# Modulation sums of an adaLN transformer: summed over partitions on TensorE beside the projections and kept on chip

## The chip, the cores and the metric

The kernel runs on one core of a Trainium2 chip. The engines of a core are named as in the profile: PE (TensorE), DVE (VectorE), ACT (ScalarE), POOL (GpSimd) and SP (SyncE, which here only issues DMAs). The metric is the device time of one execution in microseconds (us). Everything is computed in fp32.

## What is computed

512 tokens of width 1024 go through three layers: a first block (gated delta rule and spatial gating side by side, then a mixture of experts), a second layer with forgetting attention ("fox") and experts, and a third with latent attention (MLA) and experts. The second and third layer are modulated: a conditioning vector `c` gives, for each of the two layers, six rows of 1024 numbers:

```python
    c_act = jax.nn.silu(c)
    for i in range(DEPTH_2):
        mod = c_act @ w_ada[i] + b_ada[i]
        sh1, sc1, g1, sh2, sc2, g2 = [m[:, None, :] for m in jnp.split(mod, 6, axis=-1)]
        h = rmsnorm(x, mix_norm[i]) * (1.0 + sc1) + sh1
...
        x = x + g1 * y
        h = rmsnorm(x, ffn_norm[i]) * (1.0 + sc2) + sh2
        x = x + g2 * hier_moe(h, moe_w_grp[i], moe_b_grp[i], moe_w_rt[i], moe_b_rt[i],
                              moe_w_gate[i], moe_w_up[i], moe_w_down[i])
```

`y` is the attention of `h` (fox in layer 0, MLA in layer 1).

`w_ada[i]` is 1024 x 6144, 25 MB a layer. These sums depend on nothing but `c` and the weights, so they can be made at any time before the layer.

## The kernel before

**The sums.** Work is cut into 48 "slabs" a layer: six sums `m` times eight blocks `k` of 128 rows. A slab is a [128, 1024] piece of `w_ada` (512 KB) that SP loads (line 262) into one of four buffers (`NA = 4`: the `state` buffer, `ada_w` and two halves of a weight ring buffer, `ring_halves` in the trace). DVE multiplies it by a column of silu(c) and adds it to an accumulator of [128, 1024] (`sum_slab`, lines 282 and 286); two accumulators alternate. After eight slabs the accumulator holds, in each of its 128 partitions, a partial sum of one modulation row; the sum over the partitions is still to be taken. SP stores it to the scratch tensor `ada_part` in DRAM (line 266).

**Where they run.** Layer 0's slabs run beside two stages of the first block: 24 beside the u/v projections (block at line 521) and 24 beside the gate projections, the spatial mixing and the output projections (block at line 637). There DVE does twelve slabs before its "gated" step (line 738) and two behind each of the first six output jobs. Layer 1's 48 run beside the fox projections (from line 2361). A job is one 128-token by 512-column output, eight fp32 products of PE into one PSUM bank (lines 531, 651, 690, 2443). Weights come in chunks through a ring of buffers; SP issues a chunk (`W.issue`, line 120) as soon as the job that used the old one is done, from the same instruction stream as the slab loads, in the order that `move_slabs` sets.

**Stages.** Each `nc.Block()` holds one instruction stream for each engine and ends with a barrier of all engines. Named steps (`PE.done`, `DV.wait` and so on) are counts on one semaphore per engine.

**The way back.** In each of the two expert stages ahead of a modulated layer, SP reloads the six partial sums (`modulation_loads`, from line 1272), and DVE adds the bias in four adds of one partition by 1536 (line 1922). In the combine stage (`Combine.sums`, line 2044) PE sums over the partitions: eight products of a full block of ones with 512 columns give the four rows that are needed in all partitions (line 2047; "rows"), and 16 products of 128x128 with one column give sh1 and sc1 as columns (line 2053; "cols"). DVE copies the columns (line 2117) and makes the scales (lines 2119, 2122); PE's `turn(0)`, the transposes (line 2072), waits for these and for ACT's normed rows (line 2099).

## Time and profile before

| | us |
|---|---|
| median of 3 runs | 2089.75 |
| lowest, highest | 2088.21, 2093.47 |
| span of the profiled execution | 2089.7 |
| PE busy in it | 2004.7 |
| DVE busy | 965.4 |
| ACT busy | 441.4 |
| POOL busy | 361.3 |

The profiled execution is as long as the median run. A "busy" figure says how long an engine worked, not whether anyone waited for it; for that the rows below give windows of single stages, and timelines with the idle time before an instruction and its releaser in square brackets. A row of a timeline may join several equal instructions (x4); an fp32 product of PE shows as two records.

### The profile page before, as it was taken

What the parts mean: (1) busy time and instruction counts of PE and PEld (TensorE: products, weight loads), DVE (VectorE), ACT (ScalarE), POOL (GpSimd) and SP (SyncE); (2) the same over time, 40 slices, a digit from 0 to 9 for tenths busy, and PEclk for the clock granted to TensorE, in tenths of its full rate; (3) what the DMA queues carried; (4) which work ended last, traced back from release to release, by engine and by line L of the source; (5) the groups of instructions that cost most, each with busy time, mean ns of one, the idle gap of its engine ahead of it and who ended that gap; (6) DMA issues with size and microseconds to landing.
All of it is one profiled execution on the core that took longest, in us unless ns stands there. A gap on an engine that the chain in (4) does not pass through costs nothing. (4 is left out here: it accounts for less than half of the span.)

```text
span 2089.7 us, 20494 instructions
## 1 busy us (share of the span) xinstructions
PE 2004.7 (96%) x7434; PEld 1071.0 (51%) x7434; DVE 965.4 (46%) x1776; ACT 441.4 (21%) x1063; POOL 361.3 (17%) x540
## 2 busy tenths in 40 slices
PE   8999999999999999999899999999998999999995
PEld 4444444578874444444445446454445557544442
DVE  3444534567673024333454556253344467444333
ACT  1112111023241001100241126220004446320000
POOL 1000000000002000334200026103331003203333
PEclk9999999999999999999998999999999999999997
DMA  6223365610022134699715861138994120046996
GB/s 197 81 97 131 115 248 181 212 72 2 1 65 91 66 103 161 227 408 401 293 63 210 323 220 52 44 140 318 402 393 169 64 103 1 3 161 224 373 379 243
DMA packets 125750, 367.53 MB, mean 176 GB/s; under 512 B 28028, under 2 KB 33432, under 8 KB 113104
## 3 DMA queue, kind: packets, MB, share of 16 engines
q1 hardware_dynamic: 79744, 177.28, 23.9%
q10 hardware_dynamic: 30432, 157.30, 19.3%
q0 software_dynamic: 15472, 31.61, 4.3%
q8 instruction: 62, 1.02, 0.2%
q14 instruction: 40, 0.33, 0.0%
HBM read 339.79 MB, written 43.55 MB: 183 GB/s over the span
## 5 line engine op out<-in xcount | busy, mean ns | idle before, releaser
L1640 PE MATMUL bank<-ring,work 128*128 128x512 f32 x768 | 340.3, 596 | 3.3 <-DVE work L1656 3.3
L1640 PEld LDWEIGHTS bank<-ring,work 128*128 128x128 f32 x768 | 143.1, 191 | 166.7 <-issue 166.7
L1939 POOL DMA_INDIRECT work<-x_rows,small x168 | 169.6, 1010 | 267.2 <-DVE work L1904 202.6
L1651 PE MATMUL bank<-ring_halves,work 128*128 128x512 f32 x384 | 172.8, 593 | 4.0 <-DVE work L1665 4.0
L2443 PE MATMUL bank<-ring,featT 128*128 128x512 f32 x384 | 170.0, 603 | 1.6 <-DVE small L2535 1.6
L1368 PE MATMUL bank<-ring,work 128*128 128x512 f32 x384 | 168.2, 598 | 3.0 <-PEq L1184 1.0
L432 PE MATMUL bank<-featT,ring 128*128 128x512 f32 x384 | 168.7, 593 | 2.4 <-DMA ring<-in_w_in 2.4
L1662 DVE TENSOR_TENSOR work<-work,bank 128x256 f32<-128x256 f32 x48 | 20.2, 421 | 280.1 <-ACT work L1659 280.1
L2443 PEld LDWEIGHTS bank<-ring,featT 128*128 128x128 f32 x384 | 73.9, 194 | 93.9 <-issue 92.2
L1651 PEld LDWEIGHTS bank<-ring_halves,work 128*128 128x128 f32 x384 | 72.7, 190 | 95.1 <-issue 95.1
L1368 PEld LDWEIGHTS bank<-ring,work 128*128 128x128 f32 x384 | 72.8, 192 | 92.3 <-issue 92.3
L432 PEld LDWEIGHTS bank<-featT,ring 128*128 128x128 f32 x384 | 71.2, 190 | 83.3 <-issue 80.8
L531 PE MATMUL bank<-ring,featT 128*128 128x512 f32 x256 | 110.4, 593 | 0.9 <-PEq L412 0.9
L1659 ACT ACTIVATE work<-bank 128x256 f32<-128x256 f32 x48 | 18.4, 384 | 412.6 <-PE bank L1640 412.6
L1904 DVE STREAM_TRANSPOSE work<-work 128x1024 f32<-128x1024 f32 x42 | 85.1, 2027 | 0.0
L1085 PE MATMUL bank<-ring,featT 128*128 128x512 f32 x192 | 83.3, 593 | 1.0 <-PEq L815 1.0
L531 PEld LDWEIGHTS bank<-ring,featT 128*128 128x128 f32 x256 | 48.5, 190 | 61.4 <-issue 61.4
L286 DVE SCALAR_TENSOR_TENSOR ring_halves<-ring_halves,ismall 128x1024 f32<-128x1024 f32 x48 | 61.6, 1283 | 37.6 <-DMA ring_halves<-in_w_ada 34.1
L453 DVE TENSOR_SCALAR work<-bank,small 128x512 f32<-128x512 f32 x24 | 18.0, 751 | 105.3 <-PE bank L432 105.3
L1085 PEld LDWEIGHTS bank<-ring,featT 128*128 128x128 f32 x192 | 36.1, 190 | 44.7 <-issue 44.7
L1193 PE MATMUL bank<-ring,work 128*128 128x512 f32 x128 | 55.5, 593 | 0.9 <-PEq L1074 0.9
L690 PE MATMUL bank<-ring,work 128*128 128x512 f32 x128 | 55.3, 592 | 0.0
(472 smaller groups left out, 2859.2 us busy)
## 6 DMA issues: line engine op xcount, KB each, us to landing
ring<-in_w_in SPq DMA_DIRECT2D x15, 2048.0 KB
ring<-in_moe_w_gate ACTq DMA_DIRECT2D x28, 1024.0 KB
ring<-in_moe_w_up ACTq DMA_DIRECT2D x28, 1024.0 KB
ring_halves<-in_moe_w_down ACTq DMA_DIRECT2D x28, 1024.0 KB, 10.2
ring_halves<-in_w_ada SPq DMA_DIRECT2D x48, 512.0 KB, 6.9
y_rows<-work ACTq DMA_DIRECT2D x48, 512.0 KB
ring<-in_expert_w_gate ACTq DMA_DIRECT2D x14, 1024.0 KB
ring<-in_expert_w_up ACTq DMA_DIRECT2D x14, 1024.0 KB
```

Source lines behind the costliest of these rows:

```text
L286: DV.done(nc.vector.scalar_tensor_tensor(out=acc, in0=w, scalar=c_cols[:, k:k + 1], in1=acc, op0=ALU.mult, op1=ALU.add), ("slab", i))
L432: last = nc.tensor.matmul(bank[b % 4][:, :], w[:, k, (b % 4) * P:(b % 4 + 1) * P], featT[:, k, :], start=(k == 0), stop=(k == KD - 1))
L531: last = nc.tensor.matmul(uv_bank(j)[:, :], featT[:, k, t * P:(t + 1) * P], w[:, k, :], start=(k == 0), stop=(k == KD - 1))
L690: last = nc.tensor.matmul(six(16 + j)[:, :], gatedT[:, t, k, :], w[:, k, :], start=(k == 0), stop=(k == KD - 1))
L1085: last = nc.tensor.matmul(zg_bank(j)[:, :], featT[:, k, t * P:(t + 1) * P], w[:, k, :], start=(k == 0), stop=(k == KD - 1))
L1193: last = nc.tensor.matmul(bank[j][:, :], oT[:, k, t * P:(t + 1) * P], w[:, k, :], start=(k == 0), stop=(k == KD - 1))
L1368: last = nc.tensor.matmul(bank[j % 4][:, :], outT[:, k, t * P:(t + 1) * P], w[:, k, :], start=(k == 0), stop=(k == KD - 1))
L1640: last = nc.tensor.matmul(gu_sum[par], xgT[par][:, k, :], w_gu[par][:, k, :, :], start=(k == 0), stop=(k == KD - 1))
L1651: last = nc.tensor.matmul(bank[5 + h][:, :], hT[par][:, k, :], w_dn[par][:, k, span(h)], start=(k == 0), stop=(k == KF - 1))
L1904: nc.vector.transpose(xgT[par].rearrange("p k (s b) -> p s k b", s=NQ), xg[par].rearrange("p (s a k) -> p s k a", s=NQ, k=KD)).then_inc(M_ ...
L1939: nc.gpsimd.indirect_dma_start(out=xg[par][:, s * QD:(s + 1) * QD], out_offset=None, in_=x_quarters, in_offset=bass.IndirectOffsetOnAxis(a ...
L2443: last = nc.tensor.matmul(f_bank(j)[:, :], featT[:, k, t * P:(t + 1) * P], w[:, k, :], start=(k == 0), stop=(k == KD - 1))
```

## The change

The sum over partitions is taken at once, beside the projections. After certain jobs PE multiplies each half of a finished accumulator by a 32-column block of ones (`mod_sum`): two products of [128, 512] into 32 PSUM partitions each, of bank 0 (bank 7 in the fox stage, whose projections now rotate through six banks instead of seven). So every row arrives in 32 equal copies. DVE adds the bias to 64 partitions x 512 (`keep_mod`) and keeps the result in a small on-chip tensor (`mod_all`, 1040 columns) or, for sh1 and sc1, in a piece of a work buffer. The bias was loaded there before by eight DMAs of POOL (`load_mod_bias`). POOL turns sh1 and sc1 into columns with 16 DMAs of 128 elements a layer (`store_mod_cols`). The scratch tensor, its stores and reloads, the bias adds of the expert stages and the column products of the combine stages are gone. The rows of the combine stage are products with one partition of ones. `ada_w` is no longer a buffer, so slabs go through three (`NA = 3`); the position of the weight chunks among the slab loads moves by up to one slab with it. In the fox stage the slabs run over jobs 4 to 21 instead of 4 to 23.

```diff
-        ada_w = [state, sb("ada_w", [P, KD * P]), ring[3][:, 0:DM], ring[3][:, DM:2 * DM]]
+        ada_w = [state, ring[3][:, 0:DM], ring[3][:, DM:2 * DM]]
...
+        mod_rows = mod_all[:, 0:2 * BANK].rearrange("p (b n) -> p b n", b=2)
+        sh_cols, sc_cols = (mod_all[:, 2 * BANK + KD * i:2 * BANK + KD * (i + 1)] for i in range(2))
...
-        def store_sum(eng, i):
-            l, q = i // SLABS, i % SLABS // KD
-            eng.dma_start(ada_part[l, :, q * DM:(q + 1) * DM], ada_acc(i)).then_inc(ada_stored[i // KD % 2], 16)
 
...
             if k == 0:
                 if i >= 2 * KD:
-                    dve.wait_ge(ada_stored[i // KD % 2], 16 * (i // KD // 2))
+                    dve.wait_ge(PE.sem, mod_summed[i // KD - 2])
...
-                if j >= NA and beside[j - NA] % KD == KD - 1:
-                    store_sum(sp, beside[j - NA])
                 for _ in range(issue_after.count(j)):
                     W.issue(sp, 1)
-            if n and (beside[-1] + 1) % SLABS == 0:
-                for stored in ada_stored:
-                    sp.wait_ge(stored, 16 * SUMS // 2 * (beside[-1] // SLABS + 1))
+
+        def mod_sum(pe, m, b):
+            pe.wait_ge(DV.sem, slab_at[m * KD + KD - 1])
+            for h in range(2):
+                lo = 32 * (2 * (m % 2) + h)
+                last = nc.tensor.matmul(b[lo:lo + 32, :], ones[:, 0:32], ada_acc(m * KD)[:, span(h)], start=True, stop=True)
+            PE.done(last, ("mod", m))
+
+        def mod_half(m, cols):
+            q = m % SUMS
+            rows_ = slice(64 * (q % 2), 64 * (q % 2) + 64)
+            return cols[rows_, :] if q < COL_SUMS else mod_rows[rows_, (q - COL_SUMS) // 2, :]
+
+        def keep_mod(dve, m, b, cols):
+            out = mod_half(m, cols)
+            dve.wait_ge(PE.sem, mod_summed[m])
+            dve.wait_ge(mod_bias_landed[m // SUMS], 16 * 8)
+            DV.done(nc.vector.tensor_tensor(out, b[64 * (m % 2):64 * (m % 2) + 64, :], out, ALU.add), ("mod", m))
+
+        def load_mod_bias(eng, l, cols):
+            bias = D["b_ada_2"][l:l + 1, :]
+            for j in range(4):
+                eng.dma_start(cols[32 * j:32 * j + 32, :], bias[:, j * BANK:(j + 1) * BANK].partition_broadcast(32)).then_inc(mod_bias_landed[l], 16)
+                eng.dma_start(mod_rows[32 * j:32 * j + 32, :, :],
+                              bias[:, COL_SUMS * DM:].rearrange("o (b j n) -> o j b n", b=2, j=4)[:, j, :, :].partition_broadcast(32)).then_inc(mod_bias_landed[l], 16)
+
+        def store_mod_cols(eng, l, cols):
+            for m in range(l * SUMS, l * SUMS + COL_SUMS):
+                eng.wait_ge(DV.sem, mod_kept[m])
+            for i, to in enumerate((sh_cols, sc_cols)):
+                for k in range(KD):
+                    row = 32 * (2 * i + k // 4)
...
+        mod_after = {7: 0, 12: 1}
...
+                    if j in mod_after:
+                        AC.wait(pe, "beta")
+                        DV.wait(pe, "dt")
+                        mod_sum(pe, mod_after[j], bank[0])
...
-                for i in beside:
+                for i in beside[:2 * KD]:
                     sum_slab(dve, i, beside)
+                keep_mod(dve, 0, bank[0], mod_cols)
+                for i in beside[2 * KD:]:
+                    sum_slab(dve, i, beside)
+                keep_mod(dve, 1, bank[0], mod_cols)
+
+            @block.gpsimd
+            def _(pool):
+                load_mod_bias(pool, 0, mod_cols)
+                store_mod_cols(pool, 0, mod_cols)
...
+        MOD_AT = 1
+        mod_out = {2: 3, 3: 4, 7: 5}
...
+        mod_kept_at = {3: 3, 5: 4, 7: 5}
...
+                pe.wait_ge(DV.sem, mod_kept[1])
...
+                    if j == MOD_AT:
+                        DV.wait(pe, ("spT", 0))
+                        mod_sum(pe, 2, bank[0])
...
+                    if j in mod_out:
+                        AC.wait(pe, ("kept", T - 1))
+                        if mod_out[j] == 5:
+                            DV.wait(pe, ("mod", 3))
+                        mod_sum(pe, mod_out[j], bank[0])
...
-            for stored in ada_stored:
-                sp.wait_ge(stored, 16 * SUMS // 2 * (l + 1))
-            for i in range(SUMS):
-                paced(i)
-                load(sp, ada_sum[:, i * DM:(i + 1) * DM], ada_part[l, :, i * DM:(i + 1) * DM])
-            paced(SUMS)
...
-                        if mod is not None and BIAS_AT <= e < BIAS_AT + 4:
-                            i = e - BIAS_AT
-                            part = ada_sum[32 * i:32 * i + 1, i * B_ADA:(i + 1) * B_ADA]
-                            dve.wait_ge(loaded, mod_loads)
-                            DV.done(nc.vector.tensor_tensor(part, part, b_ada[32 * i:32 * i + 1, :], ALU.add), ("bias", i))
...
-                    at = ROW_OF[i][1] * DM + ROW_OF[i][2] * BANK
-                    PE.done(nc.tensor.matmul(row_bank(i)[:, :], ones[:, :], ada_sum[:, at:at + BANK], start=True, stop=True), ("row", i))
-                pe.wait_ge(loaded, self.rows.mod_loads)
+                    at = 2 * (ROW_OF[i][1] - COL_SUMS) + ROW_OF[i][2]
+                    p = 32 * (at % 4)
+                    PE.done(nc.tensor.matmul(row_bank(i)[:, :], ones[p:p + 1, :], mod_rows[p:p + 1, at // 4, :], start=True, stop=True), ("row", i))
+                pe.wait_ge(DV.sem, mod_kept[SUMS * self.rows.mod + SUMS - 1])
                 for i in range(2, len(ROW_OF)):
                     row(i)
-                for q in range(2):
-                    for k in range(KD):
-                        last = nc.tensor.matmul(bank[0][:, q * KD + k:q * KD + k + 1], ada_sum[:, q * DM + k * P:q * DM + (k + 1) * P], ones[:, 0:1], start=True, stop=True)
-                PE.done(last, "cols")
                 row(0)
...
-                dve.wait_ge(PE.sem, PE.value("cols"))
-                DV.done(nc.vector.tensor_copy(small[:, 80:80 + 2 * KD], bank[0][:, 0:2 * KD]), "cols")
-                dve.wait_ge(DV.sem, DV.value("cols"))
+                dve.wait_ge(norm_landed[self.rows.mod], 16 * (KD + 1))
+                dve.wait_ge(mod_cols_landed, 16 * COL_SUMS * KD * (self.rows.mod + 1))
...
-        f_bank = lambda j: bank[1 + j % 4] if j < 8 else bank[1 + j % 7]
-        bank_user = lambda j: j - 4 if j < 8 else {8: 5, 9: 6, 10: 7, 11: 7, 12: 7, 13: 7, 14: 4}.get(j, j - 7)
+        f_bank = lambda j: bank[1 + j % 4] if j < 8 else bank[1 + j % 6]
+        bank_user = lambda j: j - 4 if j < 8 else {8: 6, 9: 7, 10: 7, 11: 7, 12: 4, 13: 5}.get(j, j - 6)
...
-        part = lambda j: beside[SLABS * max(0, j - SLABS_AT) // (len(jobs) - SLABS_AT):SLABS * max(0, j + 1 - SLABS_AT) // (len(jobs) - SLABS_AT)]
+        SLAB_JOBS = len(jobs) - SLABS_AT - 2
+        by_job = lambda j: min(SLABS, SLABS * max(0, j - SLABS_AT) // SLAB_JOBS)
+        part = lambda j: beside[by_job(j):by_job(j + 1)]
+        mod_bank, mod_cols = bank[7], work[:, FOX_END:FOX_END + BANK]
+        mod_after = {next(j for j in range(len(jobs)) if by_job(j) >= KD * (q + 1)): SUMS + q for q in range(SUMS)}
+        mod_kept_at = {min(j + 1, len(jobs) - 1): m for j, m in mod_after.items()}
...
+                    if j in mod_after:
+                        m = mod_after[j]
+                        if m >= SUMS + 2:
+                            DV.wait(pe, ("mod", m - 2))
+                        mod_sum(pe, m, mod_bank)
...
+                PE.wait(pool, ("row", 1))
+                DV.wait(pool, ("bias", T - 1))
+                load_mod_bias(pool, 1, mod_cols)
...
+                AC.wait(pool, ("kept", T - 1, 3))
+                DV.wait(pool, ("kept", T - 1, 7))
+                store_mod_cols(pool, 1, mod_cols)
```

In the u/v stage PE's stream had sixteen jobs in a row (here jobs 6 to 13; `ring` is the weight buffer, `featT` the tokens).

Before:

```order
L531 MATMUL bank7<-ring1,featT 128x512 x8
L531 MATMUL bank1<-ring1,featT 128x512 x8
L531 MATMUL bank2<-ring0,featT 128x512 x8
L531 MATMUL bank3<-ring0,featT 128x512 x8
L531 MATMUL bank4<-ring0,featT 128x512 x8
L531 MATMUL bank5<-ring0,featT 128x512 x8
L531 MATMUL bank6<-ring1,featT 128x512 x8
L531 MATMUL bank7<-ring1,featT 128x512 x8
```

After:

```order
L573 MATMUL bank7<-ring1,featT 128x512 x8
L573 MATMUL bank1<-ring1,featT 128x512 x8
L315 MATMUL bank0<-ring_halves,ones 32x512 x2
L573 MATMUL bank2<-ring0,featT 128x512 x8
L573 MATMUL bank3<-ring0,featT 128x512 x8
L573 MATMUL bank4<-ring0,featT 128x512 x8
L573 MATMUL bank5<-ring0,featT 128x512 x8
L573 MATMUL bank6<-ring1,featT 128x512 x8
L315 MATMUL bank0<-ring_halves,ones 32x512 x2
L573 MATMUL bank7<-ring1,featT 128x512 x8
```

Two pairs of 32-column products now stand behind jobs 7 and 12; each waits for DVE's last slab of its sum, and the following job is queued behind it.

POOL had nothing in the u/v and gate stages. Before, from its last stores of the stage ahead to the delta rule (`y_rows` is another scratch tensor):

```order
L487 DMA y_rows<-work 128x1024 [waits pe_steps,pool_steps]
L487 DMA y_rows<-work 128x1024 [waits pe_steps] x6
L412 UNCONDITIONAL_BRANCH
L1031 UNCONDITIONAL_BRANCH [waits barrier_Pool_Activation_PE_DVE_SP_gather]
L1033 MEMSET state 128x1024
```

After (the four pairs of bias loads are cut to two):

```order
L450 UNCONDITIONAL_BRANCH
L631 UNCONDITIONAL_BRANCH [waits barrier_Pool_Activation_PE_DVE_SP_gather]
L332 DMA work<-in_b_ada_2 32x512
L333 DMA mod_all<-in_b_ada_2 32x2x512
...
L332 DMA work<-in_b_ada_2 32x512
L333 DMA mod_all<-in_b_ada_2 32x2x512
L342 DMA mod_all<-work 128x1x1 [waits dve_steps]
L342 DMA mod_all<-work 128x1x1 x15
L563 UNCONDITIONAL_BRANCH
L1106 UNCONDITIONAL_BRANCH [waits barrier_Pool_Activation_PE_DVE_SP_gather]
L1108 MEMSET state 128x1024
```

The bias loads and the 16 column stores now stand between two barriers; the first column store waits for DVE's two kept sums.

PE's stream in the fox combine (`work` holds the reloaded sums, `mod_all` the kept rows). Before:

```order
L2047 MATMUL bank6<-work,ones 128x512
L2053 MATMUL bank0<-ones,work 128x1 x16
L2047 MATMUL bank7<-work,ones 128x512
L2047 MATMUL bank1<-work,ones 128x512
L2062 MATMUL bank2<-level_mask,ident 128x512 x2
L2072 MATMUL bank5<-ident,work 128x128 x4
L2072 MATMUL bank6<-ident,work 128x128 x4
```

After:

```order
L2103 MATMUL bank6<-mod_all,ones 128x512
L2103 MATMUL bank7<-mod_all,ones 128x512
L2103 MATMUL bank1<-mod_all,ones 128x512
L2114 MATMUL bank2<-level_mask,ident 128x512 x2
L2124 MATMUL bank5<-ident,work 128x128 x4
```

The 16 column products between the rows are gone, and the transposes (`bank5<-ident,work`) follow the same rows as before.

## Rows read from the trace of the kernel before

**Rows 1.** The page's first part: busy us, share of the span, instructions by engine

```profile
PE 2004.7 (96%) x7434; PEld 1071.0 (51%) x7434; DVE 965.4 (46%) x1776; ACT 441.4 (21%) x1063; POOL 361.3 (17%) x540
```

**Rows 2.** Windows of three stages: us, busy (x) by engine, PEclk, DMA share, GB/s

```profile
199.00:309.00 110.00, 109.95 (x259) 48.80 (x260) 58.28 (x57) 14.75 (x28) 0.00 (x0) 1.00 0.53 189
865.00:970.00 105.00, 105.00 (x261) 47.30 (x260) 33.89 (x40) 9.82 (x20) 39.98 (x40) 1.00 1.01 396
1055.00:1233.00 178.00, 176.45 (x475) 86.09 (x473) 91.26 (x103) 33.58 (x73) 2.76 (x5) 0.96 0.63 225
```

**Rows 3.** Groups by line and form: line engine op, out<-in, shapes, count | busy us, mean ns

```profile
L531 PE MATMUL bank<-ring,featT 128*128 128x512 f32 x256 | 110.4, 593 | 0.9 <-PEq L412 0.9
...
L442 PE MATMUL bank<-featT,work 128*16 128x512 f32 x16 | 7.0, 593 | 0.0
```

**Rows 4.** Timeline of PE, second attention heads: start us, us, line, op, count

```profile
1252.95 1.13 PE L2671 MATMUL bank<-work 64*128 64x512 f32 x4
1254.02 0.44 PE L2680 MATMUL bank<-ident,ring_halves 128*128 128x128 f32 x2
```

**Rows 5.** Timeline of POOL from the first projections to the delta rule

```profile
435.51 0.95 POOL L1033 MEMSET state<- 128x1024 f32 x1 [266.48 <-POOLq L637]
```

**Rows 6.** Timeline of all engines where the u/v stage ends

```profile
309.73 0.60 ACT L603 ACTIVATE work<-bank 128x512 f32<-128x512 f32 x1 [6.27 <-PE bank L531]
...
310.64 1.06 PE L642 MATMUL bank<-ident,resid 128*128 128x128 f32 x8 [0.94 <-PEq L521]
```

**Rows 7.** Timeline of SP's queue in the u/v stage

```profile
282.26 0.38 SPq L120 DMA_DIRECT2D ring<-in_w_in  x1
...
296.18 1.72 SPq L262 DMA_DIRECT2D ring_halves<-in_w_ada  x2
```

**Rows 8.** Timeline of DVE in the u/v stage

```profile
294.86 2.67 DVE L286 SCALAR_TENSOR_TENSOR ring_halves<-ring_halves,ismall 128x1024 f32<-128x1024 f32 x2 [11.53 <-DMA ring_halves<-in_w_ada]
...
301.39 2.67 DVE L286 SCALAR_TENSOR_TENSOR ring_halves<-ring_halves,ismall 128x1024 f32<-128x1024 f32 x2
```

**Rows 9.** Timeline of POOL in the fox stage

```profile
1179.16 2.21 POOL L2362 DMA_DIRECT2D work<-key_rows  x4 [5.31 <-DMA key_rows<-work]
```

**Rows 10.** Timeline of all engines, MLA combine

```profile
1591.25 3.98 PE L2053 MATMUL bank<-ones,work 128*128 128x1 f32 x32
...
1591.97 0.95 POOL L2036 DMA_INDIRECT work<-y_rows,ismall  x1 [0.30 <-issue]
...
1593.22 0.94 POOL L2036 DMA_INDIRECT work<-y_rows,ismall  x1 [0.30 <-issue]
...
1598.95 1.15 ACT L2099 ACTIVATE work<-resid,small 128x1024 f32<-128x1024 f32 x1
...
1601.18 1.94 PE L2072 MATMUL bank<-ident,work 128*128 128x128 f32 x8 [2.33 <-DVE work L2122]
```

**Rows 11.** Timeline of DVE in the gate stage

```profile
363.23 1.28 DVE L286 SCALAR_TENSOR_TENSOR ring_halves<-ring_halves,ismall 128x1024 f32<-128x1024 f32 x1 [5.39 <-DMA ring_halves<-in_w_ada]
364.50 0.75 DVE L282 TENSOR_SCALAR ring_halves<-state,ismall 128x1024 f32<-128x1024 f32 x1
...
370.43 4.22 DVE L738 SCALAR_TENSOR_TENSOR work<-bank,small,work 128x128 f32<-128x128 f32 x16
```

**Rows 12.** Timeline of PE in the gate stage

```profile
371.60 0.66 PE L662 MATMUL bank<-ident,work 128*128 128x128 f32 x4 [1.39 <-DVE work L738]
```

**Rows 13.** Slab loads (line 262), all of the run

```profile
DMA to landing us min/median/max: 3.5/6.8/15.7
```

**Rows 14.** Timeline of DVE in the fox stage

```profile
1189.29 1.28 DVE L286 SCALAR_TENSOR_TENSOR ring_halves<-ring_halves,ismall 128x1024 f32<-128x1024 f32 x1 [4.29 <-DMA ring_halves<-in_w_ada]
...
1221.38 1.28 DVE L286 SCALAR_TENSOR_TENSOR ring_halves<-ring_halves,ismall 128x1024 f32<-128x1024 f32 x1 [5.27 <-DMA ring_halves<-in_w_ada]
```

**Rows 15.** Timeline of PE, fox combine

```profile
1030.46 3.63 PE L2053 MATMUL bank<-ones,work 128*128 128x1 f32 x32
...
1042.95 1.94 PE L2072 MATMUL bank<-ident,work 128*128 128x128 f32 x8 [3.63 <-ACT work L2099]
```

More of the change, by code:

```diff
@@ L57, in wait @@
         eng.wait_ge(self.sem, self.value(name, i))
[L60 removed]
+Rows = namedtuple("Rows", "nth index late w1 w2 mod y_in early")
 class Weights:
@@ L274, in take_slabs, with mod_names, note_steps @@
             return beside
+        def mod_names(*which):
+            return [("mod", m) for m in which]
+        def note_steps(beside, summed, kept):
+            for i in beside:
+                slab_at[i] = DV.value(("slab", i))
+            for m in summed:
+                mod_summed[m] = PE.value(("mod", m))
+            for m in kept:
+                mod_kept[m] = DV.value(("mod", m))
         def sum_slab(dve, i, beside):
@@ L317, in links @@
             return [(name, i) for i in range(n)]
-        def span(t, half=BANK):
-            return slice(t * half, (t + 1) * half)
         x_tok = D["x"][0].rearrange("(t p) n -> p t n", p=P)
@@ L519, in build @@
         ac_names = ["ab", "beta", "log_beta", "exp", "rate"] + [(s, i) for i in range(2) for s in ("log", "inv")] + ["log"] + [("drained",) + j for j in jobs]
-        stage([("sum",) + jobs[0]] + ["ab"] + [("sum",) + j for j in jobs[1:]], ac_names, dv_names + slab_names(beside))
+        mod_after = {7: 0, 12: 1}
+        mod_cols = buf[5][:, 7 * BANK:8 * BANK]
+        uv_pe = [x for j, job in enumerate(jobs) for x in [("sum",) + job] + (["ab"] if j == 0 else []) + (mod_names(mod_after[j]) if j in mod_after else [])]
+        stage(uv_pe, ac_names, dv_names + slab_names(beside[:2 * KD]) + mod_names(0) + slab_names(beside[2 * KD:]) + mod_names(1))
+        note_steps(beside, (0, 1), (0, 1))
         with nc.Block() as block:
@@ L620, in build @@
         vrstd = small[:, 128 + 14 * T:128 + 15 * T]
-        pe_names = [("spT", h) for h in range(2)] + [("sum",) + j for j in gate_jobs]
+        MOD_AT = 1
+        mod_out = {2: 3, 3: 4, 7: 5}
+        pe_names = [("spT", h) for h in range(2)] + [x for j, job in enumerate(gate_jobs) for x in [("sum",) + job] + (mod_names(2) if j == MOD_AT else [])]
         for t in range(T + 1):
@@ L625, in build @@
             pe_names += [("turned", t - 1, h) for h in range(2)] if t else []
[L626 to L627 removed]
+        pe_names += [x for j in range(OUT_EARLY, 2 * T) for x in [("out",) + gate_jobs[j]] + (mod_names(mod_out[j]) if j in mod_out else [])]
+        dv_names = [("spT", h) for h in range(2)] + [(w, t) for t in range(T) for w in ("half0", "half1")] + [("mean", t) for t in range(T)] + ["eps"] + mod_names(2)
         dv_names += [(w, t) for t in range(T) for w in ("gain", "bias")] + slab_names(beside[:12])
@@ L1333, in moe @@
             dv_n += links("route", N_ROUTE) + links("pick", N_PICK) + links("rows", N_ROWS)[:ROWS_FIRST] + ["slot_tok", "skip", "slot_f"] + links("rows", N_ROWS)[ROWS_FIRST:] + ["part_f", "part_rows"] + links("weight", N_WEIGHT)
-            dv_n += [("bias", i) for i in range(4)] if mod is not None else []
-            BIAS_AT = NE - 4
             stage([("sum", j) for j in range(6)] + [("turned", 0, 0), ("turned", 0, 1), ("sum", 6), ("turned", 1, 0), ("turned", 1, 1), ("sum", 7)] +
@@ L1996, in sum_names @@
             def sum_names(self):
-                return [("row", i) for i in range(2, len(ROW_OF))] + ["cols", ("row", 0), ("row", 1)]
+                return [("row", i) for i in range(2, len(ROW_OF))] + [("row", 0), ("row", 1)]
             def turn_names(self, t):
```

52 lines of the change are left out of this document (31 added, 21 removed).

## The prediction

> **What bounds the kernel now.** I read the busy table first: TensorE (PE) is busy for 2004.7 of 2089.7 us, 96% [rows 1]. Such a share is a mean over stages, so next come windows over the stages that the change touches. In the u/v projection stage PE is busy for 109.95 of 110.00 us, and in the projections of the first attention layer (fox) for 176.45 of 178.00; the clock is granted at or close to full, the DMA engines are at 0.53 and 0.63 of their time and DVE is at about half [rows 2]. So whatever is put on PE there lengthens the run by its own duration, and whatever is taken from DVE or the DMA queues gives nothing. The expert stage, from which the change takes six reloads, is also 105.00 of 105.00 PE, but its DMA share is 1.01 at 396 GB/s: two candidates for its pace [rows 2].
>
> **Part 1: twelve sums over partitions on PE.** Each is a pair of fp32 products of a 32-column block of ones with 512 columns, put on different column groups of the array. The trace has no 32-column product. An ordinary 512-column product is two records of 110.4/256 = 0.43 us, and a 16-column-wide one costs the same, 7.0/16 = 0.44 a record [rows 3]: narrowness alone saves nothing. What can save is that the pair runs side by side. The nearest row is the attention's pair of 64-row tiles with 512 columns: four records start at 1252.95 and the next instruction starts at 1254.02, 1.07 us for what would be 4 x 0.43 = 1.72 in a row [rows 4]. I take 1.07, as it is also a pair of 512 columns in separate parts of the array, entered from and left to full-size products. The ends are 0.86 (perfect overlap) and 1.72 (none). All twelve stand between projection or output jobs of stages where PE has no idle time, so all of it counts: 12 x 1.07 = **+12.8** (10.3 to 20.6).
> The Trainium skill, page "TensorEngine Tiling (Array Packing)", section Key Properties, says that changing the tiling mode, not just the tile, drains TensorE; the 0.21 us by which the pair of [rows 4] exceeds 0.86 would be that drain. Its page "TensorE: Matmul & The Clock Gate", section "Measured speedup vs the span model", gives a pack of tiles the time of one product plus some ns for each further tile; by that the pair would be an estimated 0.86 and the total 2106.8.
>
> **Part 2: the end of the u/v stage.** Every stage ends with a barrier of all engines. Before, POOL has nothing there (idle for 266.48 us before 435.51) and the last drain of ACT, 309.73 + 0.60, releases PE at 310.64 [rows 5, 6]. Now POOL waits there for the second kept sum, which stands on DVE behind slab 23, and then issues 16 small DMAs in front of the barrier. With three buffers slab 23 is later. The weight chunk that SP issues at 282.26 waits for a projection job, and only behind it go the loads of slabs 18 and on [rows 7]; DVE then waits until 294.86 [rows 8]. One product moves this to 295.9. Slabs 18 to 20 are summed until 299.9 (1.28 and a gap of 0.1 each). The load of 23 now needs the buffer of 20; before, with four buffers, the pair issued at 296.18 was summed from 301.39 on, so a landing took some 5 us [rows 7, 8]. So 23 lands at about 305.2, is summed at 306.5, and the bias add (64 x 512) ends at 307.2. The 16 issues go by POOL's direct DMAs: four in 2.21, so 0.55 each [rows 9]: 8.8, end 316.0. PE and ACT themselves come to 310.33 + 2 x 1.07 = 312.5. The tail is **+3.5** (0 if slab and issues run ahead; +14.7 if an issue takes the 1.25 us that separates the indirect ones, 1591.97 to 1593.22 [rows 10]).
>
> **Part 3: three slab buffers in the gate stage.** The mixing of the first token tile waits for DVE, which does twelve slabs first: they end as DVE's "gated" step begins, 370.43, and PE idles 1.39 for it [rows 11, 12]. The last five slabs come in a burst from 363.23. With three buffers the last two of the five are only issued when the first two are summed, at 364.5 and 365.2, and take the slabs' median landing of 6.8 us [rows 13]: one after the other summed by 374.2 (371.6 + 2 x 1.28), 3.7 later, of which one product on PE (1.07) covers a part: 2.6. By the shortest landing, 3.5, nothing is lost. Fewer loads in flight make each somewhat quicker, so I take **+2.0** (0 to 2.6).
>
> **Part 4: PE's waits for slabs in the fox stage.** PE now waits at six places for the eighth slab of a sum, with the next projection job queued behind it. The slabs end one job (about 7 us) ahead of each product, which hides most. Against it: DVE already waits for landings of up to 4.29 and 5.27 there [rows 14], six weight chunks block SP in between, and there is one buffer less. I estimate four of six late by half a us or so, **+2.3**; 0 if the spare job covers all, 9.6 if two are late by those two waits.
>
> **Part 5: the combine stages.** The 16 column products (32 records) go: 3.63 and 3.98 us of PE [rows 10, 15]. In the fox one PE then waits 3.63 anyway for ACT's normed rows (1042.95): gain 0 [rows 15]. In the MLA one PE waits until 1601.18 for DVE's scale rows, which stood behind the column products; ACT is done at 1598.95 + 1.15 = 1600.10, and that is late next: **-1.0** [rows 10]. The row products stay eight, each with one row of ones instead of 128; the time goes with the columns, so I give them nothing.
>
> **Part 6: what costs or gives nothing.** The eight bias adds on DVE in the expert stages, 12 stores and 12 reloads lie beside PE work that fills the stages [rows 2]. The twelve adds on DVE replace them. POOL's stores for the second layer are issued in the fox stage after its key rows, around 1182, and need 8.8 us: over long before the stage ends.
>
> **Sum.** 12.8 + 3.5 + 2.0 + 2.3 - 1.0 = +19.6, on the profiled execution's 2089.7, which is the median of the runs (2089.75): **2109.3**. This case by itself spans 2103 to 2114.
>
> **Rivals.**
> (a) The pair runs one product after the other, as two records of 0.43 each in a row do [rows 3]: 12 x 0.65 = 7.8 more, 2117.1. For it: they use the same rows and the same moving port. Against: the pair of row tiles does overlap [rows 4]. 0.10.
> (b) POOL's issues cost 1.25 each: 11.2 more, 2120.5. For: they write single elements to 128 partitions. Against: its direct DMAs take 0.55 [rows 9]. 0.11.
> (c) Three buffers set the pace of the fox stage: 9.6 in place of 2.3, 2116.6. 0.06.
> (d) Faster, the other side: the DMA engines, not PE, pace the two expert stages. The reloads are 6 x 0.52 = 3.1 MB in each, 7.9 us at 396 GB/s. If both give that back, both column blocks count (7.6) and none of the new stalls appears: 2089.7 + 12.8 - 15.9 - 7.6 = 2079.0. It decides from the point where PE would have idle time in that stage; it has none there, 105.00 of 105.00 [rows 2]. 0.04.
> (e) No change to speak of: the relief comes in one expert stage only and the stalls stay hidden: 2089.7 + 12.8 - 7.9 - 1.0 = 2093.6. Nearly the same time results if the products do not do what they say and slip into PE's gaps; the 0.05 us of idle in the u/v stage leaves no gaps [rows 2]. 0.07.
> The forecast keeps 0.62.
>
> **How the numbers follow.** About 0.3%, 6.3 us, is what can be told from no change. Faster 0.04 (d), same 0.07 (e), slower the rest, 0.89. All terms at their low ends give 2089.7 + 10.3 - 1.0 = 2099.0; I set the low end at 2096, where case (e) begins, and the high end at 2122, over (a), (b) and (c) each alone. Left out are (d), (e) and two of the high cases together, 0.15.
>
> **What would show it.** The profile after: 48 records of ones products with 32 columns on PE, and 1.07 us from the first record of a pair to the next job (0.86 or 1.72 for the ends); the u/v stage about 5.6 longer, with POOL's last column store ending after ACT's last drain; PE's idle time before the first mixing transposes grown from 1.39 to about 3.4; small idle entries before the fox products with DVE's slab sums as releaser; PE waiting for ACT, not DVE, before the MLA combine's transposes; the expert stage unchanged at 105.00 of PE work. What would make the prediction wrong: a shorter expert stage, column stores that take over 1 us each, or pairs that don't overlap.

## The result, and the profile after

The changed kernel took 2125.87 us (median of 4, 2122.04 to 2130.73) against 2088.98 for the kernel before (2083.9 to 2093.47): a ratio of 1.0182, interval 1.0159 to 1.0206. It is slower by 36.9 us, where +19.6 was forecast; the time lies 4 us above the range.

The page's first part of the changed kernel, which answers to [rows 1] (2004.7 us, 96%):

```profile
span 2128.7 us, 20503 instructions
...
PE 2009.1 (94%) x7418; PEld 1063.9 (50%) x7418; DVE 959.4 (45%) x1778; ACT 440.4 (21%) x1063; POOL 380.9 (18%) x588
```

The span is 39.0 longer, PE's busy time only 4.4: the new products and half-speed stretches came on, the column products went, and so did most of the time of the row products. PE waits 34.6 us more. Some 16 of these stand in the two combine stages, where they fill the place of products that are gone (below); the others lengthen the run, and they are what to look for. The first PE instruction behind each stage barrier gives the length of the stages (differences of such starts, in us; three of the experiments below stand beside):

| stage | before | changed | stores later | ten slabs | before, three buffers |
|---|---|---|---|---|---|
| u/v projections | 111.60 | 123.62 | 113.95 | 113.95 | 111.59 |
| gate, mixing, output | 124.91 | 136.98 | 133.92 | 127.22 | 129.85 |
| delta rule (first part) | 181.28 | 181.28 | 181.28 | 181.29 | 181.28 |
| first experts | 259.05 | 260.46 | 257.32 | 257.16 | 257.52 |
| fox combine and projections | 210.64 | 217.83 | 219.96 | 219.43 | 214.49 |
| last experts to the end | 280.56 | 285.41 | 284.89 | 281.15 | 283.90 |

+12.0, +12.1 and +7.2 in the three stages that hold the products: 31.3. The other 7.7 us stand elsewhere: 4.9 in the last stage, 1.9 ahead of the u/v stage, 1.4 in the first experts, -0.5 in the rest. The profile of before has the shortest last stage of all eleven profiles, and the granted clock says most of why. Windows, columns as in [rows 2], first of before, then of the changed kernel:

```profile
1809.14:2065.00 255.86, 250.24 (x698) 117.86 (x698) 93.78 (x154) 22.44 (x50) 68.93 (x86) 1.00 0.72 267
...
1927.20:1934.00 6.80, 5.97 (x11) 2.50 (x10) 4.24 (x19) 2.30 (x4) 4.02 (x4) 0.50 0.13 38
```

The changed kernel has a stretch of 6.8 us at half speed in the last stage, before has none there. PE is busy for 5.97 of it, so it costs 3.0 of the 4.9. Such a stretch also stands in the last stage of two kernels that are before with a small edit (1895.0 to 1901.9 and 1900.9 to 1907.7); it is not shown to come from the change.

**The end of the u/v stage.** Timeline of all engines of the changed kernel, in answer to [rows 6] (PE went on at 310.64, idle 0.94):

```profile
308.88 8.63 POOL L342 DMA_DIRECT2D mod_all<-work  x16 [103.31 <-DVE work L327]
314.02 0.60 ACT L658 ACTIVATE work<-bank 128x512 f32<-128x512 f32 x1 [6.27 <-PE bank L573]
314.08 0.38 SPq L120 DMA_DIRECT2D ring<-in_w_in  x1
...
324.60 1.94 PE L702 MATMUL bank<-ident,resid 128*128 128x128 f32 x8 [10.62 <-PEq L563]
```

POOL's 16 issues end at 317.51, ACT's drain at 314.62, and yet PE goes on at 324.60, 7.1 us after that; in these no engine works. The column stores' own rows of the last two issues say when their data arrived (6.1 us behind the issue, 323 for the last):

```profile
L342 POOL DMA_DIRECT2D mod_all<-work x2: 544/544/544, 316.4 to 317.0; - x2
...
DMA to landing us min/median/max: 5.9/6.1/6.3
```

**The clock behind the waits.** Windows of the changed kernel, columns as in [rows 2]:

```profile
201.00:311.00 110.00, 110.00 (x262) 47.90 (x263) 59.61 (x59) 14.71 (x28) 6.27 (x12) 1.00 0.55 181
316.00:324.00 8.00, 0.00 (x0) 0.00 (x0) 0.00 (x0) 0.00 (x0) 1.51 (x3) 0.51 0.68 236
324.00:328.00 4.00, 3.40 (x10) 2.44 (x11) 2.11 (x4) 1.28 (x1) 0.00 (x0) 0.50 0.65 202
328.00:330.00 2.00, 2.00 (x4) 0.87 (x3) 2.00 (x4) 0.00 (x0) 0.00 (x0) 0.56 0.98 401
392.00:398.00 6.00, 6.00 (x28) 5.68 (x29) 5.16 (x19) 0.60 (x1) 0.00 (x0) 0.50 1.04 400
891.00:996.00 105.00, 105.00 (x261) 47.22 (x260) 33.86 (x40) 9.80 (x20) 39.73 (x40) 1.00 0.99 367
```

The granted clock is 0.50 (1.2 of 2.4 GHz) until about 330, after a wait of 10.6 us, and again from 392 to 398, after one of 4.1. PE counts as busy there, at half speed. The expert stage is what it was, 105.00 of 105.00 PE, with 367 GB/s instead of 396.

**The gate stage.** DVE and PE, from two timelines, in answer to [rows 11, 12] (gated step at 370.43, PE idle 1.39):

```profile
379.65 1.28 DVE L299 SCALAR_TENSOR_TENSOR ring_halves<-state,ismall,ring_halves 128x1024 f32<-128x1024 f32 x1 [5.75 <-DMA state<-in_w_ada]
...
390.79 4.22 DVE L807 SCALAR_TENSOR_TENSOR work<-bank,small,work 128x128 f32<-128x128 f32 x16
```

```profile
341.87 1.05 PE L315 MATMUL bank<-ring_halves,ones 128*32 128x512 f32 x4
342.85 41.47 PE L711 MATMUL bank<-ring,featT 128*128 128x512 f32 x96
...
391.96 2.15 PE L725 MATMUL bank<-ident,work 128*128 128x128 f32 x8 [4.08 <-DVE work L807]
393.90 3.62 PE L736 MATMUL bank<-work,resid 128*128 128x128 f32 x16
```

From the first record of a pair to the next product it is 342.85 - 341.87 = 0.98 us. That is not yet the price of a pair: the records on both sides of it also stand further apart (0.52 and 0.53 instead of 0.43), and the first experiment gives 1.18 from the length of a stage. PE then waits 4.08 for DVE's gated step, which waits for slabs; the 16 records that took 1.95 take 3.62.

**The MLA combine**, PE's timeline, in answer to [rows 10]:

```profile
1635.32 1.94 PE L2124 MATMUL bank<-ident,work 128*128 128x128 f32 x8 [10.35 <-ACT work L2151]
1637.05 3.58 PE L2114 MATMUL bank<-level_mask,ident 128*128 128x512 f32 x4
1640.47 4.05 PE L2947 MATMUL bank<-ring,featT 128*128 128x288 f32 x16
```

**The fox stage**, PE's waits ahead of its products, two rows of PE's timeline:

```profile
1215.51 1.05 PE L315 MATMUL bank<-ring_halves,ones 128*32 128x512 f32 x4 [1.88 <-DVE small L2620]
...
1237.97 1.05 PE L315 MATMUL bank<-ring_halves,ones 128*32 128x512 f32 x4 [0.62 <-DVE ring_halves L299]
```

At 1215.51 the profile names L2620, DVE's instruction just behind the last slab; that slab itself had waited 1.12 for its load. The other four pairs are not waited for.

The granted clock falls in this stage in both kernels, at the same place, with PE busy all the time. Before, then the changed kernel:

```profile
1109.70:1123.30 13.60, 13.60 (x46) 10.40 (x46) 0.74 (x1) 0.00 (x0) 0.00 (x0) 0.50 0.41 142
...
1138.70:1148.90 10.20, 10.20 (x35) 7.62 (x35) 1.29 (x1) 0.00 (x0) 0.00 (x0) 0.50 0.34 106
```

The stretch is 3.4 us shorter in the changed kernel, which gives back 1.7. Its combine also brings the first job 0.5 earlier (22.44 us behind the stage's start instead of 22.91).

### The profile page after: what moved, and what is told of

Read it like the earlier page. It is cut to its first block and busy times, and to the rows that moved or that the text cites. A ratio compares the mean times of both kernels' runs of the same rounds, so it can differ in the third digit from the quotient of the medians.

```text
span 2128.7 us, 20503 instructions
## 1 busy us (share of the span) xinstructions
PE 2009.1 (94%) x7418; PEld 1063.9 (50%) x7418; DVE 959.4 (45%) x1778; ACT 440.4 (21%) x1063; POOL 380.9 (18%) x588
## 5 line engine op out<-in xcount | busy, mean ns | idle before, releaser
L1702 PE MATMUL bank<-ring,work 128*128 128x512 f32 x768 | 345.8, 604 | 3.3 <-DVE work L1718 3.3
L2502 PE MATMUL bank<-ring,featT 128*128 128x512 f32 x384 | 169.8, 601 | 1.6 <-DVE small L2599 1.6
L1430 PE MATMUL bank<-ring,work 128*128 128x512 f32 x384 | 166.5, 593 | 3.0 <-PEq L1259 1.1
L573 PE MATMUL bank<-ring,featT 128*128 128x512 f32 x256 | 110.9, 594 | 0.9 <-PEq L450 0.9
L299 DVE SCALAR_TENSOR_TENSOR ring_halves<-ring_halves,ismall 128x1024 f32<-128x1024 f32 x56 | 71.8, 1282 | 34.0 <-DMA ring_halves<-in_w_ada 31.2
L1160 PE MATMUL bank<-ring,featT 128*128 128x512 f32 x192 | 83.3, 592 | 1.0 <-PEq L888 1.0
L299 DVE SCALAR_TENSOR_TENSOR ring_halves<-state,ismall,ring_halves 128x1024 f32<-128x1024 f32 x28 | 35.9, 1283 | 58.9 <-DMA state<-in_w_ada 57.8
L711 PE MATMUL bank<-ring,featT 128*128 128x512 f32 x128 | 57.1, 607 | 0.0
```

The costliest lines, as they stand in the source:

```text
L299: DV.done(nc.vector.scalar_tensor_tensor(out=acc, in0=w, scalar=c_cols[:, k:k + 1], in1=acc, op0=ALU.mult, op1=ALU.add), ("slab", i))
L573: last = nc.tensor.matmul(uv_bank(j)[:, :], featT[:, k, t * P:(t + 1) * P], w[:, k, :], start=(k == 0), stop=(k == KD - 1))
L711: last = nc.tensor.matmul(six(j)[:, :], featT[:, k, t * P:(t + 1) * P], w[:, k, :], start=(k == 0), stop=(k == KD - 1))
L1160: last = nc.tensor.matmul(zg_bank(j)[:, :], featT[:, k, t * P:(t + 1) * P], w[:, k, :], start=(k == 0), stop=(k == KD - 1))
L1430: last = nc.tensor.matmul(bank[j % 4][:, :], outT[:, k, t * P:(t + 1) * P], w[:, k, :], start=(k == 0), stop=(k == KD - 1))
L1702: last = nc.tensor.matmul(gu_sum[par], xgT[par][:, k, :], w_gu[par][:, k, :, :], start=(k == 0), stop=(k == KD - 1))
```

## The experiments

The theory after the two traces: (A) POOL does not reach the stage barrier before its own small DMAs have landed, and these share the DMA engines with the 2 MB weight chunk; (C) three slab buffers hold up DVE in the gate stage; (E) the products take 0.98 a pair, from the first record to the next product, since column groups overlap; and each PE wait of some us costs as much again in half-speed clock.

### Column stores in the gate stage

```diff
             def _(pool):
                 load_mod_bias(pool, 0, mod_cols)
-                store_mod_cols(pool, 0, mod_cols)
...
+            @block.gpsimd
+            def _(pool):
+                store_mod_cols(pool, 0, mod_cols)
```

The added lines stand in the gate stage's block.

> The changed kernel with one edit: the 16 column stores of the second layer's modulation (POOL) are issued in the gate stage and no longer in the u/v stage. Theory A (the tail of the u/v stage is POOL's alone): PE's idle time before the gate stage falls from 10.6 to about 1 us, and the slow clock after it (17.3 us for what took 14.7) goes with it: 9.7 + 2.6 = 12.3 us, so about 2113.6 us, a ratio to the kernel before of 1.012. Rival B (the stage end waits for something else that the change brought, such as the later slabs or SP's weight chunk): the idle time stays above 5 us and the run above 2119 us.

Measured: 2112.62 (2112.26 to 2114.68), ratio 1.0118, interval 1.0087 to 1.0149; 13.3 under the changed kernel. Its timeline of all engines:

```profile
312.63 1.06 PE L701 MATMUL bank<-ident,resid 128*128 128x128 f32 x8 [0.94 <-PEq L563]
...
313.16 4.96 POOL L342 DMA_DIRECT2D mod_all<-work  x9 [109.87 <-POOLq L563]
```

The wait is back at 0.94 and the half-speed stretch is gone (L701 takes 1.06, not 1.94). The u/v stage is 113.95 against 111.60 before, both with 0.94 of idle time at its end: its two pairs cost 2.35, 1.18 each. Theory A stands: the whole tail was the column stores.

### The weight chunk behind the barrier

```diff
-                move_slabs(sp, beside, [NA - 1] + spread(24, 3))
-                W.issue(sp)
+                move_slabs(sp, beside, [NA - 1] + spread(24, 3)[:2])
...
+                W.issue(sp, 1)
                 move_slabs(sp, beside, spread(24, 4))
```

> The changed kernel with the 2 MB weight chunk, which SP issues at the end of the u/v stage, issued as the first instruction of the gate stage. The changed kernel's last column store ends at 317.5 and PE goes on at 324.6, 7.1 us later. Theory A1 (POOL's stream reaches the barrier only when its own small DMAs have landed, and these lie in the DMA engines behind the 2 MB chunk): the 7.1 falls to 2 to 3 us. Rival A2 (each store really costs POOL about 0.96 us, 16 x 0.96 = 15.4 from 308.9 to 324.3, whatever the trace shows): it stays at 7. Rival A3 (a fixed time of POOL behind its last store): it stays at 7.

Measured: one run, 2115.34. Timeline of all engines, and the landing of the last two stores:

```profile
308.77 8.63 POOL L342 DMA_DIRECT2D mod_all<-work  x16 [103.34 <-DVE work L327]
...
320.02 0.38 SPq L120 DMA_DIRECT2D ring<-in_w_in  x1
...
320.08 1.94 PE L701 MATMUL bank<-ident,resid 128*128 128x128 f32 x8 [6.25 <-PEq L563]
```

```profile
DMA to landing us min/median/max: 1.9/1.9/1.9
```

From the last issue's end, 317.40, to PE it is 2.7 us and no longer 7.1, as A1 said. POOL's 16 issues are the same, so neither a hidden price of the issue (A2) nor a fixed time behind it (A3) explains the 7.1. What changed is the landing: 1.9 us instead of 6.1.

### Half of the stores

Eight column stores in the u/v stage, eight in the gate stage:

```diff
                 load_mod_bias(pool, 0, mod_cols)
-                store_mod_cols(pool, 0, mod_cols)
+                store_mod_cols(pool, 0, mod_cols, (0,))
...
+                store_mod_cols(pool, 0, mod_cols, (1,))
```

> The changed kernel with 8 of the 16 column stores in the u/v stage and the other 8 in the gate stage. The 8 start about 308.9 and their last ends about 313.3; ACT's last drain ends at 314.6 and the weight chunk moves data from 315 on. Theory A1 (landing behind the chunk): they have landed before it, and PE goes on at 315 to 315.5, idle about 1 to 1.5 us. A2 (0.96 us each): POOL is through at 316.6, PE goes on at about 316.9. A3 (fixed 7 us behind the last store): 320.3.

Measured: one run, 2128.26. None of the three numbers came: DVE was later here, so the stores started at 310.52 and ended behind the chunk's issue.

```profile
310.52 4.35 POOL L343 DMA_DIRECT2D mod_all<-work  x8 [105.44 <-DVE work L327]
...
313.57 0.38 SPq L120 DMA_DIRECT2D ring<-in_w_in  x1
...
322.02 1.94 PE L703 MATMUL bank<-ident,resid 128*128 128x128 f32 x8 [8.54 <-PEq L564]
```

```profile
DMA to landing us min/median/max: 6.1/6.4/6.7
```

Read by the mechanism and not by the numbers: the last two stores, issued up to 314.3, took 6.1 and 6.7 to land, 321.0, and PE went on at 322.02. Half as many stores shorten the wait by 2.1 us only (8.54 against 10.62). A2, counted from the real start, would give 318.2. By itself this run can't tell A1 from A3; with the one before it can.

### One small DMA in the kernel before

```diff
+            @block.gpsimd
+            def _(pool):
+                AC.wait(pool, ("drained",) + jobs[-1])
+                pool.dma_start(probe[:, :], ident[0:1, :]).then_inc(probed, 16)
```

> The kernel before with one small DMA more and nothing else: in the u/v stage POOL waits for ACT's last drain (310.3) and writes 128 numbers of 4 bytes to a scratch tensor, in front of the stage's barrier; SP has issued the 2 MB weight chunk 0.6 us earlier. Theory A1 (POOL reaches the barrier only when its own DMA has landed, here behind the chunk): PE, which went on at 310.6 before, goes on at 317 to 321. Rival A3 in a mild form (POOL only needs the 0.55 us of the issue): at 311.2 to 311.5.

Measured: one run, 2103.24. All engines, and the landing of the added DMA, then of the chunk:

```profile
311.34 0.38 SPq L120 DMA_DIRECT2D ring<-in_w_in  x1
311.35 0.60 ACT L605 ACTIVATE work<-bank 128x512 f32<-128x512 f32 x1 [6.27 <-PE bank L533]
312.23 0.52 POOL L610 DMA_DIRECT2D probe<-ident  x1 [141.60 <-ACTq L523]
...
319.90 1.94 PE L649 MATMUL bank<-ident,resid 128*128 128x128 f32 x8 [8.60 <-PEq L523]
```

```profile
DMA to landing us min/median/max: 7.3/7.3/7.3
...
DMA to landing us min/median/max: 11.0/11.0/11.0
```

A single transfer of 512 bytes holds all five engines for 7.6 us: issued at 312.23, landed at 319.5, PE on at 319.90, against 0.94 of idle time without it. This is theory A alone, in the kernel before.
Nobody waits for the semaphore of that DMA. The Trainium skill, page "DMA: Bandwidth & Descriptors", section "Queues, rings and completion order", says that a DMA engine takes turns between queues packet by packet; so a small transfer need not wait for the whole chunk. Here it did not: issued 0.9 us behind the chunk, it landed at 319.5, some 2.8 us ahead of it. But its 7.3 us are far from the 1.9 of the stores without a chunk; what held it for that long, no run here shows.

### The stores issued by ACT

The 16 stores stand on ACT between its last two drains, with a semaphore of their own:

```diff
                 for j, (n, t) in enumerate(jobs):
+                    if j == len(jobs) - 1:
+                        store_mod_cols(act, 0, mod_cols)
                     PE.wait(act, ("sum", n, t))
```

> The changed kernel with the 16 column stores of the u/v stage issued by ACT instead of POOL, between its last two drains (16 issues of some 0.35 us from about 308.3, through at 314), with a semaphore of their own; they still stand in front of the stage's barrier, and the last of them still land behind the start of the 2 MB chunk. Theory A4 (only POOL's own DMAs hold its way to the barrier; those that ACT issues through a hardware queue do not): PE goes on at 315 to 316.5, idle 1 to 2.5 us in place of 10.6, and the run is near the 2112.6 of the first experiment. Rival A5 (the barrier waits for small DMAs of any engine, or for this transfer): PE goes on at 322 to 325.

Measured: 2124.85 (2119.97 to 2127.55), ratio 1.0174, interval 1.0141 to 1.0208. All engines, and the landing of the last two stores:

```profile
308.83 12.49 ACTq L342 DMA_DIRECT2D mod_all<-work  x16
...
321.37 0.60 ACT L659 ACTIVATE work<-bank 128x512 f32<-128x512 f32 x1 [14.12 <-issue]
...
322.28 1.94 PE L703 MATMUL bank<-ident,resid 128*128 128x128 f32 x8 [8.80 <-PEq L563]
```

```profile
DMA to landing us min/median/max: 5.0/5.2/5.4
```

The time by PE (322.28) looks like rival A5, but the rows say something else. The issues took 12.49 / 16 = 0.78 us each, not 0.35, so ACT's own drain is late, 321.97. PE goes on 0.3 us behind that, while the last store, issued about 320.7, lands only near 326. So transfers that ACT issues do not hold the barrier; these were dear for another reason, their issue. The expected gain missed by the issue price.

### Both products of a pair on one column group

```diff
-                lo = 32 * (2 * (m % 2) + h)
+                lo = 32 * (2 * (m % 2))
```

> The changed kernel with both 32-column products of a pair on the same column group (the same 32 PSUM partitions; the second overwrites the first, so half of each modulation row is lost and the output is wrong). In the changed kernel a pair takes 0.98 us from its first record to the next instruction. Theory E (they take 0.98 because two column groups run side by side): now 1.7 to 1.8. Rival F (a 32-column product is simply cheaper, 0.25 a record): still 0.98.

Measured, PE's timeline:

```profile
256.84 1.90 PE L315 MATMUL bank<-ring_halves,ones 128*32 128x512 f32 x4
258.68 34.60 PE L573 MATMUL bank<-ring,featT 128*128 128x512 f32 x80
```

1.84 for the pair instead of 0.98 (one run, 2139.44). Theory E: the two column groups do run side by side, and that saves 0.86 a pair. The stage agrees: its length less PE's wait at its end is 114.72 (127.50 - 12.78) against 113.00 (123.62 - 10.62), 0.86 for each of its two pairs.

### Narrow products

```diff
-                last = nc.tensor.matmul(b[lo:lo + 32, :], ones[:, 0:32], ada_acc(m * KD)[:, span(h)], start=True, stop=True)
+                last = nc.tensor.matmul(b[lo:lo + 32, 0:16], ones[:, 0:32], ada_acc(m * KD)[:, h * BANK:h * BANK + 16], start=True, stop=True)
```

> The changed kernel with the 24 products over 16 columns of the accumulator in place of 512 (the rest of each modulation row is not computed; same waits, same order). Theory G (the products cost their own duration, 12 x 0.98 = 11.8, on top of everything else): with some 0.1 to 0.2 left for each pair, 9.5 to 10.5 us less than the changed kernel, about 2116. Rival H (the products fall partly into time that PE would wait anyway, for slabs in the fox and gate stage): 7 us less or fewer.

Measured: 2117.89 (2113.68 to 2121.93), ratio 1.0126, interval 1.0096 to 1.0156: 8.0 less than the changed kernel, between the two theories.

```profile
255.89 0.24 PE L315 MATMUL bank<-ring_halves,ones 128*32 128x16 f32 x4
256.06 34.60 PE L573 MATMUL bank<-ring,featT 128*128 128x512 f32 x80
```

A pair is 0.17 now, so 12 x 0.81 = 9.7 are gone from PE. In this profile the u/v tail was 2.2 us longer (idle 12.82), and in the fox stage the clock fell at one more place, so only part shows. By its median the run does not decide between G and H. The u/v stage does for its two pairs: its length less the wait at its end is 111.39 (124.21 - 12.82) against 113.00, 0.81 less a pair, that is in full, as G says. The waits for slabs in the fox stage stayed what they were (2.37 and 0.54 against 1.88 and 0.62), which also speaks against H.

### Three buffers in the kernel before

```diff
-        ada_w = [state, sb("ada_w", [P, KD * P]), ring[3][:, 0:DM], ring[3][:, DM:2 * DM]]
+        ada_w = [state, ring[3][:, 0:DM], ring[3][:, DM:2 * DM]]
```

> The kernel before with three slab buffers instead of four (the buffer ada_w left out of the list) and nothing else. Theory C (the third of the loss in the gate stage comes from the buffers): PE's wait for DVE's gated step grows from 1.8 us in all to about 4, the clock falls to half behind it, and the run is 4 to 6 us slower, about 2094, ratio 1.002 to 1.003; the fox stage does not change. Rival D (the late slabs in the gate stage come from the products, the kept adds and the half-speed start, not from the buffers): within 1 us of the kernel before, PE's wait stays under 2 us.

Measured: 2099.58 (2097.17 to 2113.36), ratio 1.0069, interval 1.0041 to 1.0096: more than either theory said. PE's timelines of the gate stage, and at the end of the fox stage:

```profile
375.06 2.15 PE L662 MATMUL bank<-ident,work 128*128 128x128 f32 x8 [4.79 <-DVE work L738]
...
1241.49 2.89 PE L2636 MATMUL bank<-ident,work 128*128 128x128 f32 x12 [6.61 <-PEq L2396]
```

In the gate stage it is theory C to the letter: the wait grows from 1.8 to 4.8, half speed behind it, +4.9 for the stage. The fox stage was expected unchanged and is not: DVE's last slab ends at 1237.85, 3.0 behind PE's last job, the store of its sum lands 3.0 us behind its issue at 1237.9, and PE waits 6.61 at the barrier, +3.9 for the stage. The changed kernel waits 0.94 there; its slabs end two jobs earlier and the store is gone. Which of the two matters was not run. The seven runs spread over 16 us, more than those of any other kernel here.

### Ten slabs ahead of the gated step

With the stores in the gate stage as above:

```diff
-        out_slabs = lambda j: beside[12 + 2 * j:14 + 2 * j] if j < 6 else ()
+        out_slabs = lambda j: beside[10 + 2 * j:12 + 2 * j] if j < 7 else ()
...
-        mod_out = {2: 3, 3: 4, 7: 5}
+        mod_out = {2: 3, 4: 4, 7: 5}
...
-                for i in beside[:12]:
+                for i in beside[:10]:
```

> The changed kernel with the column stores in the gate stage (as in the first experiment, 2112.6) and ten slabs instead of twelve ahead of DVE's gated step; the other fourteen stand two by two behind seven output jobs, and the fifth pair of products one job later. Theory C (three buffers make the slabs late there, PE waits 4.1 us, and the half-speed clock behind the wait costs some 2 more): the wait falls under 1.5 and the half-speed stretch goes, 4 to 6 us less than the first experiment, about 2107.6. Rival: the stream of slabs is late anyway and holds the later products instead, 2112 to 2113.

Measured: 2104.14 (2101.07 to 2106.68), ratio 1.0065, interval 1.0042 to 1.0087: 8.5 under the first experiment. PE's timeline:

```profile
312.95 1.06 PE L701 MATMUL bank<-ident,resid 128*128 128x128 f32 x8 [0.94 <-PEq L563]
...
327.68 1.05 PE L315 MATMUL bank<-ring_halves,ones 128*32 128x512 f32 x4
...
373.54 1.04 PE L724 MATMUL bank<-ident,work 128*128 128x128 f32 x8
...
379.79 5.75 PE L752 MATMUL bank<-ring,work 128*128 128x512 f32 x13
```

No wait before the first mixing transposes, and no half speed. The gate stage is 127.22: 124.91, less the 1.8 that PE waited before, plus four pairs (4.7), is 127.8, 0.6 over it. The stage gained 6.7 on the first experiment, where 4 to 6 were expected; what the two profiles differ by beyond that is mostly the last stage, 3.7, of which a shorter half-speed stretch makes 1.5. This is the best form of the change that was run, and it still loses 13.5 us to the kernel before (2090.68 in the same series), near the price of its twelve pairs, 14.1.

## Why the prediction was wrong

The direction was right, the size was not, and none of the rivals (a) to (e) happened. Step by step:

- **Part 1, the products: right mechanism, a little too small.** By the forecast's own measure, first record to next product, 1.07 was taken and 0.98 measured. But that measure leaves out the wider spacing on both sides; and the pair of [rows 4] isn't entered from full-size products, as the working has it, but from products of 64 output rows (line 2659). By the length of the u/v stage a pair costs 1.18, twelve 14.1 instead of 12.8. The 0.86 of a perfect overlap is missed by 0.32. Rival (a) has its number too, 1.84 by the first measure.
- **Part 2, the tail: the step that failed.** Its pieces were good: last slab done at 307.5 (306.5 forecast), kept add at 308.3 (307.2), 16 issues in 8.63 (8.8). The working then took the end of the last issue for the end of POOL's stage. It is not: the barrier opens when POOL's own DMAs have landed, 6.1 us later behind a 2 MB chunk. The tail was 9.7 and not 3.5. The chunk's row was in the trace of before (SP issues one at 309.73, as the last job ends), and long landings too (up to 15.7 us for slabs [rows 13]); only the link from landing to barrier was missing.
- **The clock was in no term.** A wait was priced at its length. The wait of 10.6 was followed by half speed until 330: from the stage's first PE instruction to its first pair 17.27 us, against 14.73 in the run without the wait, +2.5. The wait of 4.1 in the gate stage cost another 2.7 (from the transposes to the first output job 9.24, against 6.92 before, of which 0.38 was a second wait).
- **Part 3, the buffers: right mechanism, too small.** PE's idle time went up by 2.3 (2.0 forecast); with the clock it is 5.0. The three-buffer run shows that the buffers alone do it (+4.9 for the stage).
- **Part 4: the number right, the way to it in part luck.** 1.88 + 0.62 = 2.5 against 2.3, but from two late pairs and not four, one of them late by far more than half a us; with small edits the two waits were 2.63 and 0.79 (first experiment).
- **Part 5: right at its place, void behind it.** The row products did not stay as they were: 14 records of one partition take 2.00 us in the fox combine, where 12 of 128 partitions took 7.08 (5.39 in the MLA one). The forecast gave them nothing; it changed nothing either, since PE then waits for ACT, 9.49 and 10.35 us. The MLA transposes start 14.10 behind the stage's start instead of 15.15, the forecast 1.0. But PE had now idled 10.35 us, its next four products took 3.58 instead of 2.73 at the lower clock, and the next job starts only 0.2 earlier.

The sum of what was measured in the three stages: pairs 14.1, tail 9.7 and half speed behind it 2.5, gate wait 2.3 and half speed behind it 2.7, fox waits 2.5, less 0.5 in the fox combine and 1.7 for its shorter half-speed stretch, is 31.6; the stages show 31.3. The profiles differ by 39.0, the medians by 36.9 (interval 33 to 43). The rest sits in stages where the forecast had nothing and that vary from run to run: the last is 280.56 in the profile of before and 281.1 to 285.4 in ten others, two of them the kernel before with a small edit. Half-speed stretches explain most of it in the profiles: 3.0 of 4.9 in the last stage, 1.7 of 1.9 ahead of the u/v stage, 1.3 of 1.4 in the first experts. Why they stand in one run and not in another stays open. The range failed for the same reason as the sum: its upper end looked for a dearer issue, not for a landing.

## What to carry to other kernels

In these kernels a DMA that POOL issues ahead of a barrier of all engines costs its landing, not its issue, and the landing is longest when a large load is issued at that moment: put such stores at the start of the next stage, where 16 of them showed no cost. Price a wait of TensorE of several us with the half-speed stretch behind it, 1.9 to 2.7 us here. Price an added product by the length of a stage, not by the distance to the next instruction. And an added operation on the engine that is the bound needs a saving on the same engine: here relieved DMA queues and DVE gave nothing back, and neither did PE's own savings in the combine stages, since ACT was late there.

## What the runs showed of the hardware

- The barrier opened (by PE's next start) 0.4 to 1.5 us behind the landing of POOL's last DMA in four kernels (landings 1.9 to 7.3 us after the issue), with no wait on that DMA's semaphore in the program at that place. For DMAs issued by ACT it did not wait.
- A column store (512 bytes in 128 elements) took 5.9 to 6.7 us to land beside a 2 MB load, 1.9 without it; the one small DMA in the kernel before took 7.3 beside it.
- The same column store costs 0.54 us to issue on POOL and 0.78 on ACT.
- A pair of 32-column fp32 products (512 columns each) on two column groups lengthened a stage by 1.18 us, on one column group by 2.03.
- Fourteen records of fp32 products with one partition and 512 columns took 2.00 us, twelve with 128 partitions 5.39, both at the full clock. Neighbours of the first kind read different partitions (0, 32, 64, 96); whether that is why they are so short was not run.
- TensorE's granted clock was 0.50 after waits of 10.6, 4.1 and 4.8 us, and after 2.2 to 2.6 us in the fox stage of four experiments; it stayed at 1.00 after the 1.88 of the changed kernel and the 1.39 and 2.40 (at 15.38) of the kernel before. A wait is not the only way to it: in the kernel before it fell at 1109.7 while PE had been busy all the time (with products of 16 columns from 1106.76 on), and stayed at 0.50 until 1123.3.
